# Layer 0's first three tiles on unnormalised rows, the scale half of adaLN and x loaded first

## What is computed

```python
mod_lat = silu_c @ w_ada[i] + b_ada[i]
...
shift, scale, gate = jnp.split(mod, 3, axis=-1)
h = rms_norm(x, norm_w) * (1 + scale[:, None]) + shift[:, None]
proj = h @ w_in
xbc_raw, z_m, dt_raw, u_raw, v_raw, z_g, gl_m, gl_g = jnp.split(
    proj, _split_points(IN_SIZES), axis=-1)
```

## Time and profile before

| | us |
|---|---|
| median of 3 runs | 1404.61 (1404.55 to 1405.31) |
| the profiled execution | 1405.58 |
| its span in the profile | 1403.9 |
| PE busy | 1390.7 (99%) |
| DVE busy | 1009.1 (72%) |
| POOL busy | 1026.8 (73%) |
| ACT busy | 457.9 (33%) |

### The profile page before, as it was taken

One profiled execution on the slowest core, in us unless ns is written; L12 is line 12 of the kernel. 1 busy time (PEld: TensorE's weight loads), 2 busy tenths in 40 slices (PEclk: granted clock), 3 DMA queues, 4 the chain that ended last, 5 costly groups with the idle time before them and its releaser, 6 DMA issues.

```text
span 1403.9 us, 26639 instructions
## 1 busy us (share of the span) xinstructions
PE 1390.7 (99%) x9935; PEld 1334.6 (95%) x9935; DVE 1009.1 (72%) x1484; ACT 457.9 (33%) x1021; POOL 1026.8 (73%) x1421
## 2 busy tenths in 40 slices
...
PEclk9999999999999999999999999999999999999998
...
GB/s 353 95 134 85 183 163 165 68 61 120 187 186 184 171 221 210 151 151 153 107 135 123 106 164 148 186 91 61 106 134 191 191 174 200 142 186 120 76 76 91
DMA packets 197326, 205.26 MB, mean 146 GB/s; under 512 B 76512, under 2 KB 163680, under 8 KB 195808
## 3 DMA queue, kind: packets, MB, share of 16 engines
...
...
## 4 chain that ended last, share of the span: by engine, by line
PE 98%; DMA 1%; SPq 0%; DVE 0%; issue 0%; DVEq 0%
PE acc L687 80%; PE X L654 5%; PE acc L654 3%; PE X L913 2%; PE X L893 2%; PE X L929 1%; PE X L954 1%; PE acc L807 1%; DMA ada_pre<-in_wada 1%; PE X L922 1%; PE X L766 0%; PE acc L754 0%; DVE xr L2042 0%; SPq L507 0%; PE acc L701 0%; PE X L701 0%
## 5 line engine op out<-in xcount | busy, mean ns | idle before, releaser
L588 POOL CAST w_hi<-w_st 128x256 fp32r<-128x256 f32 x696 | 412.7, 607 | 329.9 <-PE acc L687 166.8
L592 POOL TENSOR_TENSOR w_lo<-w_st,w_hi 128x256 fp32r<-128x256 f32 x696 | 643.5, 935 | 0.0
L687 PE MATMUL acc<-h_hi,w_hi 128*128 128x320 f32 x1744 | 413.8, 318 | 0.0
L687 PE MATMUL acc<-h_hi,w_lo 128*128 128x320 f32 x1744 | 397.2, 309 | 0.0
L687 PE MATMUL acc<-h_lo,w_hi 128*128 128x320 f32 x1744 | 397.1, 309 | 0.0
L687 PEld LDWEIGHTS acc<-h_hi,w_hi 128*128 128x128 f32 x1744 | 292.0, 188 | 18.8 <-issue 15.1
L687 PEld LDWEIGHTS acc<-h_lo,w_hi 128*128 128x128 f32 x1744 | 291.5, 188 | 0.0
L687 PEld LDWEIGHTS acc<-h_hi,w_lo 128*128 128x128 f32 x1744 | 291.5, 188 | 0.0
L1721 DVE SCALAR_TENSOR_TENSOR cv<-raw,convw_sb,cv 128x642 f32<-128x642 f32 x128 | 137.7, 1076 | 4.5
L1464 DVE SCALAR_TENSOR_TENSOR ada_acc<-ada_st,sc,ada_acc 128x512 f32<-128x512 f32 x112 | 107.6, 1000 | 1.8
L1203 ACT ACTIVATE cvt<-cv 128x642 f32<-128x642 f32 x32 | 23.8, 743 | 164.0 <-DVE cv L1721 164.0
...
## 6 DMA issues: line engine op xcount, KB each, us to landing
w_st<-in_wts SPq DMA_DIRECT2D x174, 512.0 KB, 3.6
...
ada_st<-in_wada SPq DMA_DIRECT2D x33, 512.0 KB, 4.3
...
ada_pre<-in_wada SPq DMA_DIRECT2D x15, 512.0 KB, 9.3
...
```

The costliest lines, as they stand in the source:

```text
L588: nc.gpsimd.tensor_copy(quarter(w_hi, slot, q), quarter(w_st, slot, q)).then_inc(s_pool, 1)
L592: nc.gpsimd.tensor_tensor(quarter(w_lo, slot, q), quarter(w_st, slot, q), f(quarter(w_hi, slot, q)), ALU.subtract).then_inc(w_split, 1)
L687: last = mm(a[:, hf, 0:n1], w[:, s, cols], x[:, k, hf * HALF:hf * HALF + n1], start=(k == 0 and n == 0), stop=(k == KC - 1 and n == 2))
```

## The change

- The two scale jobs come first, the two shift jobs last. SP loads job 0 ahead of x, x comes in four quarters, and the weights' first halves lie between them.
- Tiles 0 and 1 of layer 0 run on p (without norm and shift), in pairs of chunks as p and the weights become ready; tile 2 runs on p with the two shift columns, as in layer 1.
- For tiles 0 and 1 the shift comes from tile_shift: 64 small matmuls of the *raw* fp32 weights in w_st with the shift, into TILE_SHIFT in PSUM. ACT copies it to bsh, where raw_conv takes its bias. SP therefore waits for shift_mm before it loads the weights of tiles 2 and 3 into the same slots.
- ACT makes p_hi for k 0 to 3 ahead of the squares, and the rest behind them; DVE likewise makes p_lo. unscaled and raw_conv run in layer 0 as in layer 1. h_hi and h_lo are still made, for tile 3 on.
- keep_pace runs 14 matmuls in place of 25. Buffers of w_ada lie elsewhere; convolution 0 starts behind unscaled(2).

```diff
-JOBS_FIRST = [(0, q, h) for h in (0, 1) for q in (1, 0)]
+JOBS_FIRST = [(0, q, h) for q in (1, 0) for h in (0, 1)]
 NF = len(JOBS_FIRST)
...
-    ada_pre = place("ada_pre", [P, 4 * NF - 1, 2, 512], r_v)
+    ada_pre = [place(f"ada_pre{n}", [P, 2, 512], at) for n, at in
+               enumerate([r_h + 4096 * i for i in range(4)] + [r + 4096 * i for r in (r_v, r_r) for i in range(5)])]
...
     job_part = place("job_part", [P, 2, 16], r_ex)
     ssq = place("ssq", [P, TOK], r_cum)
+    hrows = place("hrows", [P, 4, 32], r_cum)
...
-        return acc[n][:, 0, :] if n < 2 else X[2][:, :]
+        return acc[0][:, 0, :] if n == 0 else X[2][:, :]
 
     DT_FIRST = (X[3][:, 0:HALF], X[1][:, 0:HALF], X[1][:, HALF:HALF + 2])
+    TILE_SHIFT = X[1][:, HALF + 2:HALF + 6].rearrange("p (t v) -> p t v", t=2)
...
+        def first_ada(job):
+
+            L, q, hf = JOBS_FIRST[job]
+            for n in range(4 * job, 4 * job + 4):
+                sp.dma_start(ada_first(n), wada[L, q, hf, n % 4, :, :, :]).then_inc(pre_in[n // 2], 16)
...
+        def first_x(i):
+
+            k = slice(2 * i, 2 * i + 2)
+            sp.dma_start(xr[:, k, :], xT[:, k, :]).then_inc(x_part[i] if i < len(x_part) else x_in, 16)
...
         sp.dma_start(c_sb[:, :, :], cT).then_inc(c_in, 16)
-        sp.dma_start(xr[:, 0:KC // 2, :], xT[:, 0:KC // 2, :]).then_inc(x_half, 16)
-        sp.dma_start(xr[:, KC // 2:KC, :], xT[:, KC // 2:KC, :]).then_inc(x_in, 16)
+        first_ada(0)
         sp.dma_start(bada_sb[:, :, :], bada).then_inc(norm_in, 16)
         sp.dma_start(normw_sb[:, :, :], normw).then_inc(norm_in, 16)
         sp.dma_start(ea[:, :], alog).then_inc(norm_in, 16)
-        for n in range(4 * NF):
-            L, q, hf = JOBS_FIRST[n // 4]
-            sp.dma_start(ada_first(n), wada[L, q, hf, n % 4, :, :, :]).then_inc(pre_in[n // 2], 16)
-            if n == 7:
-                dt_weight(0)
-                half_weight(0, 0)
-            if n == 11:
-                half_weight(1, 0)
+        half_weight(0, 0)
+        first_x(0)
+        first_x(1)
+        half_weight(1, 0)
+        first_x(2)
+        first_x(3)
+        first_ada(1)
         half_weight(0, 1)
         half_weight(1, 1)
+        dt_weight(0)
+        first_ada(2)
+        first_ada(3)
         load_consts()
         for t in range(2, DEPTH * NT):
             L, p = divmod(t, NT)
             sp.wait_ge(w_split, WQ * (t - 1) if t > 2 else FIRST_SPLIT[0][-1])
+            if t < 4:
+                sp.wait_ge(shift_mm, t - 1)
             weight(t, t % 2)
...
+        def tile_shift(t, half):
+
+            for k in range(KC // 2 * half, KC // 2 * (half + 1)):
+                for b in range(4):
+                    last = mm(TILE_SHIFT[32 * b:32 * b + 32, t, :], w_st[:, t, P * k + 32 * b:P * k + 32 * (b + 1)],
+                              mods[:, 0, :, k], start=False, stop=False)
+            if half == 1:
+                last.then_inc(shift_mm, 1)
+
+        def opening():
+
+            ready = (phi_ready, plo_ready, 0)
+
+            def chunks(*tk):
+                for t, k in tk:
+                    chunk(t, k, p_hi, p_lo, ready)
+
+            chunks((0, 0), (0, 1), (1, 0), (1, 1), (0, 2), (1, 2), (0, 3), (1, 3))
+            first_mm(1)
+            stat_mm(0)
+            first_tp(1)
+            chunks((0, 4), (1, 4))
+            stat_bc(0)
+            chunks((0, 5), (1, 5))
             first_mm(2, range(DTG))
-            chunk(0, 0, hi, lo, ready)
-            chunk(0, 1, hi, lo, ready)
+            chunks((0, 6), (1, 6))
             first_mm(2, range(DTG, KC))
-            chunk(0, 2, hi, lo, ready)
+            for t in range(2):
+                chunk(t, 7, p_hi, p_lo, ready).then_inc(tile_done, 1)
             first_tp(2)
-            chunk(0, 3, hi, lo, ready)
-            acc_ready(1)
-            chunk(1, 0, hi, lo)
-            first_mm(3, range(DTG))
-            chunk(1, 1, hi, lo)
-            first_mm(3, range(DTG, KC))
-            chunk(1, 2, hi, lo)
+            dt_part(0, 0)
+            first_mm(3)
+            dt_part(0, 1)
             first_tp(3)
-            dt_part(0, 1)
-            chunk(1, 3, hi, lo)
-            pe.wait_ge(job_read, NF)
+            for half in range(2):
+                pe.wait_ge(job_read, 3 + half)
+                for t in range(2):
+                    tile_shift(t, half)
             dt_shift(0)
-            for t in range(2):
-                for k in range(KC // 2, KC):
-                    last = chunk(t, k, hi, lo, ready)
-                    if (t, k) == (1, 5):
-                        dt_transposes(0)
-                last.then_inc(tile_done, 1)
 
...
-            if n >= 2:
+            if n >= 1:
...
-        keep_pace(17)
+        keep_pace(4)
         first_mm(0, range(DTG))
-        stat_mm(0)
+        keep_pace(4)
         first_mm(0, range(DTG, KC))
-        stat_bc(0)
+        keep_pace(2)
         first_tp(0)
-        first_mm(1, range(DTG))
-        keep_pace(6)
-        first_mm(1, range(DTG, KC))
-        keep_pace(2)
-        first_tp(1)
-        dt_part(0, 0)
+        keep_pace(4)
...
             if L == 0:
-                opening(*h)
+                opening()
+                pe.wait_ge(sh_ready, 2)
             else:
-                pe.wait_ge(sh_ready, 2 * L)
...
                 hooks = within(p)
-                if p == 1:
+                if p == 2 - L:
                     hooks = [(6, lambda: dt_transposes(L))]
-                raw_rows = L > 0 and p < RAWT
+                raw_rows = p < RAWT
                 rows, more = ((p_hi, p_lo), 2) if raw_rows else (h, 0)
-                ready = (hhi_ready, h_ready, L) if L > 0 and RAWT <= p < RAWT + 3 else None
+                ready = (hhi_ready, h_ready, L) if RAWT <= p < RAWT + 3 else None
...
+        def first_p(k):
+
+            act.wait_ge(amul_ready, k // (KC // 2) + 1)
+            for v, cols in ((0, slice(0, CTX)), (1, slice(CTX, TOK))):
+                last = A(p_hi[:, k, cols], xr[:, k, cols], ACT.Copy, scale=amul[:, 0, v, k:k + 1])
+            last.then_inc(phi_ready, 1)
+
+        row_copy(0)
+        for k in range(KC // 2):
+            if k % 2 == 0:
+                act.wait_ge(x_part[k // 2], 16)
+            first_p(k)
         for k in range(KC):
-            if k == KC // 2:
+            if k == 4:
+                act.wait_ge(x_part[2], 16)
+            if k == 6:
                 act.wait_ge(x_in, 16)
             square(0, k, xr[:, k, :])
         warm_root()
+        row_copy(1)
+        first_p(4)
         root(0)
-        row_copy(0)
-        act.wait_ge(rbc_ready, 1)
-        A(c_buf[4][:, 0:CTX], X[1][:, 0:P], ACT.Copy).then_inc(rs_ready, 1)
-        row_copy(1)
+        for k in range(5, KC):
+            first_p(k)
+        rs_copy(0)
 
...
             if L == 0:
-                act.wait_ge(job_read, 2)
-                for k in range(KC // 2):
-                    h_high(k)
                 row_copy(2)
                 act.wait_ge(norm_in, 48)
                 A(ea[:, :], ea[:, :], ACT.Exp).then_inc(ea_ready, 1)
+                act.wait_ge(job_read, 3)
+                h_high(0)
+                h_high(1)
                 row_copy(3)
                 act.wait_ge(job_read, NF)
-                for k in range(KC // 2, KC):
+                A(p_hi[:, :, TOK:TOK + 2], mods[:, 0, :, :].rearrange("p v k -> p k v"), ACT.Copy).then_inc(sh_ready, 1)
+                for k in range(2, 6):
                     h_high(k)
                 act.wait_ge(consts_in, 16 * 6)
                 act.wait_ge(dt_done, 1)
                 sums = dt_sums(0)
                 A(bsh[:, RAWT, :], sums[2], ACT.Identity, bias=dtb_sb[:, 0:1])
+                A(bsh[:, 0:2, :], TILE_SHIFT, ACT.Copy)
                 for hf in range(2):
                     last = A(c_buf[0][:, hf * HALF:(hf + 1) * HALF], sums[hf], ACT.Copy)
                 last.then_inc(dtrow_ready, 1)
+                act.wait_ge(pads_ready, 1)
+                act.wait_ge(dtrow_ready, 1)
+                raw_conv(0)
+                for k in range(6, KC):
+                    h_high(k)
...
-                if L == 0 or p >= RAWT:
+                if p >= RAWT:
...
+        def first_low(k):
+
+            dve.wait_ge(phi_ready, k + 1)
+            for v, cols in ((0, slice(0, CTX)), (1, slice(CTX, TOK))):
+                last = STT(out=p_lo[:, k, cols], in0=xr[:, k, cols], scalar=amul[:, 0, v, k:k + 1],
+                           in1=f(p_hi[:, k, cols]), op0=ALU.mult, op1=ALU.subtract)
+            last.then_inc(plo_ready, 1)
+
+        dve.wait_ge(norm_in, 48)
+        job_out(0)
+        for k in range(KC // 2):
+            first_low(k)
         for k in range(KC):
             add_square(0, k)
+        job_out(1)
+        first_low(4)
         rstd(0)
-        dve.wait_ge(norm_in, 48)
-        job_out(0)
+        for at in (32, 64):
+            nc.vector.memset(hrows[at:2 * at, 2:4, :], 0.0)
+        for k in range(5, KC):
+            first_low(k)
...
```

(26 more changed lines are left out.)

82 lines of the change are left out of this document (28 added, 54 removed).

## The result

The changed kernel takes 1413.45 us (median of 6 runs, 1411.93 to 1414.26), the kernel before 1404.58 us (6 runs, 1404.25 to 1405.31): ratio 1.006, 95% interval 1.005 to 1.007, **8.87 us slower**. The forecast was 1408.3, or 3.7 slower, with a range up to 1411.5: the sign is right, the size is not, and the measured time lies above the range.

The account below looks back on a forecast made before the run. PE, busy 99%, bounds the kernel. 3.5 us gained early, then weight 2's late load, its split and the lost clock put T3 at 58.9 against 55.2: +3.7, 1408.3 us; range 1405.0 to 1411.5.

Parts of the forecast that it names:

- T3: Start of PE's first matmul of tile 3, the first v tile; 55.23 us before the change, forecast about 58.9.
- POOL's first quarters: POOL's split of weight 2 ahead of tile 2: two hi quarters and the lo need 0.74 and 0.75 us.
- Loads and start of the tiles: Opening: reordered loads let chunk (0,0) start at 14.1 us, against 26.82 for the first chunk before.
- The middle: PE from about 23 us to dt_shift's end: waits, then chunks, jobs and shifts, all ending at 44.75 us.
- three stalls: PE's waits of 0.7, 0.7 and 1.7 us between job 1's halves and chunk (0,4), 3.1 us in all.
- The eight chunks: Tiles 0 and 1 on k 0 to 3: from 14.1 to 21.2 us, p_lo at 0.95 a k on DVE.
- The load behind the shift: SP issues weight 2 only after tile 0's shift, at 44.1 us; landing takes 3.6, PE idles 4.45.
- Clock in the gap: PE's idle before tile 2 likely drops its clock to the lower level, adding about 1.5 us to T3.
- PE or POOL for T3: Which limits tile 3's start: PE with the cold clock at 58.5 us or POOL's quarters at 58.7, side by side.
- What costs nothing: DVE's convolutions start some 18 us later, covered by DVE's 12.0 us idle before the fifth, at no cost.
- not slower: Rival: squares done by 23.2, weight 2 issued at 41.0, T3 at 53.9; 1.3 us faster, 1403.3; chance 0.1.
- The second rival: The clock also falls in the middle, slowing chunks on k 4 to 7; +5 to +7 us, 1411; chance 0.13.

Follow-up runs that it names:

- e2: The changed kernel with six matmuls nobody reads put into PE's waits between job 1 and chunk (0,4); 1411.47 us, ratio 1.0046.
- e8: The changed kernel with DVE waiting ahead of h_low(0) until POOL has split the first quarter of weight 2; 1412.77 us, ratio 1.0057.
- e1: The changed kernel with raw weights of tiles 0 and 1 in places of their own, so SP doesn't wait for the shift products; 1407.29 us, ratio 1.0018.
- e3: The changed kernel with 14 matmuls nobody reads in PE's wait between the shift products and tile 2; 1412.27 us, ratio 1.0055.
- e4: The changed kernel with ACT's job 1 row copy and p_hi(4) before the root's table load, job 1's transposes before PE's sums of squares; 1411.81 us, ratio 1.0051.
- e11: The changed kernel with eight idle repeats of the first convolution's first product on DVE; 1418.36 us, ratio 1.0093.
- e5: e1 with DVE and ACT reordered around tile 2: unscaled(0) directly behind job 2's sum, raw_conv(0) two h_high earlier; 1408.31 us, ratio 1.0026.
- e6: e5 with the middle reordered: job 1's products between chunks on k 2 and 3, ACT and DVE orders following; 1407.08 us, ratio 1.0017.
- e9: e6 with DVE's before(2) to (4) ahead of job 2's sum and before(5) to (7) ahead of job 3's; 1403.66 us, ratio 0.9991.
- e10: e9 with all eight squares and sums ahead of job 1's row and sum, sum-of-squares products behind job 1's transposes; 1403.03 us, ratio 0.9988.

## Why the prediction was wrong, step by step

The forecast put T3 at 58.9; it is 64.29, 5.4 later. By the terms of the sum:

| term | forecast | measured | error |
|---|---|---|---|
| chunk (0,0) starts | 14.1 | 14.09 | 0 |
| chunks on k 0 to 3 end | 21.2 | 22.66 | 1.5 |
| chunk (0,4) starts | 27.1 | 28.89 | 1.8 |
| dt_shift ends | 44.75 | 47.35 | 2.6 |
| weight 2 issued | 44.1 | 47.05 | 2.95 |
| its landing | 3.6 | 4.2 | 0.6 |
| first quarters to PE's start | 1.5 | 3.4 | 1.9 |
| PE idle | 4.45 | 7.31 | 2.9 |
| tile 2 to T3 | 9.7 | 9.63 | -0.1 |

The errors that make up the 5.4 are these: the eight chunks' own pace 1.5, the stalls 0.3, the way from chunk (0,4) to the dt_shift's end 0.8, the issue 0.35, the landing 0.6, POOL's first quarters 1.9, less 0.1 behind them. So two steps of the sum failed: it put the clock in the middle at nothing, where it costs 2.0 us, and POOL's first quarter of weight 2 at its quiet price, which was 1.8 us too little. The pace of the first eight chunks was mis-sized besides, by 1.5.

- **Loads and start of the tiles: right.** The first chunk came at 14.09 where 14.1 was forecast. That it agrees to the hundredth is luck: in the other eleven traces it is at 13.95 to 15.04.
- **The middle: a step that failed.** The three stalls are where they were put and sum to 3.37 us, forecast 3.1. But the sum took all PE work between them and the dt_shift at full pace and put the clock at nothing. That the clock falls there was a rival with a chance of 0.13; it was the fact (0.55 and 0.50 in its rows), and e2 measures it at 2.0 us. The table shows only 0.8 of this, since two terms were too dear: p_lo(4) did not come late (0.5), and the 64 shift products took about 1.2 us and not 1.84. That shorter burst is also why weight 2's issue stood 0.3 ahead of the dt_shift's end and not 0.65.
- **The eight chunks: mis-sized by 1.5 us.** DVE's p_lo was late twice. Its rows have 1.27 us a k (5.07 for four) where I had put its quiet 0.95; POOL was splitting weights beside it. That POOL slowed it here is argued from e8, not tested.
- **The load behind the shift: right in kind.** e1 measures it with all that hangs on it at 6.2 us, of which the forecast had 4.45 of idle time and 1.55 of clock.
- **POOL's first quarters: the other step that failed.** The sum took 0.74 and 0.75 from rows in which DVE was not at h_lo, for a stretch of which the same section says that DVE is not quiet. The price of contention was put on POOL's path to tile 3 only, 11.0 us for seven quarters, but not on the first one, which PE waits for. It was 1.8 us (e8: 2.51 against 0.74). That is its price in this trace, not a fixed one: where DVE pays in POOL's place, as in e3 and e4, the casts take 0.85 and 0.81, and PE's wait is 5.87 (e4) instead of 7.31. The page "GPSIMD Engine Reference" of the Trainium skill (Key points) names contention with DVE instructions that have two SBUF inputs. It was cited for the other quarters, and the trace agrees for this one just as well: h_lo reads h_pre and h_hi.
- **Clock in the gap: right.** The rule cited from "TensorE: Matmul & The Clock Gate" in the Trainium skill (Why this matters for your kernels) agrees with the rows, 0.53 and 0.50. 1.55 was allowed for; tile 2 with the dt transposes took 9.63 instead of 7.77, 1.9 more, of which e3 gave back 1.2. Long rests are not the only ones that cost it: it also fell among the rests of the middle, none of them over 1.63 us.
- **PE or POOL for T3:** forecast near level, POOL just ahead; it was PE. POOL's third quarter of tile 3 was there at 63.3, 1 us ahead.
- **What costs nothing: true here, by luck.** No new wait stood behind T3. But the argument, DVE's 12 us of idle time before its fifth convolution, looked at the wrong place. The binding one is v_tok behind the fourth, where ACT ended at 102.6 and PE asked at 105.7 (e11). There 3.1 us were left. The cover held since the convolutions started 1.0 us behind T3 with PE 9 us late; with PE earlier and the convolutions 6.8 us behind T3 it was gone (e5, e6: 3.6 us with the clock). The rival "not slower", with T3 at 53.9, would likely have met this wait; it was not tried in that form.
- **The range.** Each error was within reach of a rival, but they add: a late middle makes the load late, and the clock can fall at either rest. The range treated them as alternatives. The second rival, at +5 to +7, was the nearest.

So the early start gained less than it should: PE was to be 3.5 us ahead at the dt_shift, and was 0.9 by the trace (47.35 against about 48.2). Then SP's wait for the shift, with the load and the split behind it, gave back 7.3 us of PE. With the raw weights in a place of their own and the orders of e5, e6, e9 and e10, the same idea is 1.6 us faster than before.
